# Transposing normalised rows by DMA instead of TensorE in a hybrid decoder step on eight cores

## The reference

```python
h = rmsnorm(x, g_mix);  proj = h @ w_in              # a | u | v | gate_a | gate_b
pa = pool_mixer(a)                                   # causal window means, 4 groups
u, v = gelu(u), rmsnorm(gelu(v), g_v)
sg = u * (tril(w_s) @ v + b_s)                       # per chunk of 128 rows
merged = sigmoid(gate_a) * (pa @ w_pool_out) + sigmoid(gate_b) * (sg @ w_gmlp_out)
x = x + merged @ w_out
h2 = rmsnorm(x, g_ffn)
x = x + (silu(h2 @ w_gate) * (h2 @ w_up)) @ w_down   # 2816 hidden
y = rmsnorm(x, g_final)
```

## Time and profile before

| what | value |
|---|---|
| median of 3 runs | 889.79 us (888.06 to 893.38) |
| span of the profiled execution, slowest core | 882.3 us (cores: 876.1 to 882.3) |
| PE busy | 830.3 us, 94% of the span |
| DVE / ACT / POOL busy | 366.0 / 247.1 / 142.6 us |
| PE share of the chain that ended last | 88% |
| DMA traffic | 81.05 MB, mean 92 GB/s |

### The profile page before, as it was taken

The page is one execution under the profiler, slowest core; times in us unless marked ns, Lnnn a source line. Parts: engine busy times, 40 slices in busy tenths (PEclk is TensorE's granted clock), DMA queues, the critical chain, the costliest instruction groups (busy, mean ns, idle before and its releaser), DMA issues.

```text
span 882.3 us, 13022 instructions; the slowest of 8 cores (876.1 to 882.3 us)
## 1 busy us (share of the span) xinstructions
PE 830.3 (94%) x4584; PEld 392.5 (44%) x4584; DVE 366.0 (41%) x601; ACT 247.1 (28%) x448; POOL 142.6 (16%) x174
## 2 busy tenths in 40 slices
PE   1689999999999999999997999999999999999996
PEld 1334444445444444444443444444544444444442
DVE  2448544447322211134557594434631212114446
ACT  3643422225311111120126543222441111110012
POOL 2420011021201010000225201201120101000003
PEclk9989999999999999999999999999999999999999
DMA  8995336666884746266367951567678475455304
GB/s 209 201 141 66 72 39 74 79 102 91 95 97 51 94 51 82 40 93 96 48 139 243 155 66 25 73 82 103 80 87 104 54 90 72 60 84 84 60 18 174
DMA packets 102482, 81.05 MB, mean 92 GB/s; under 512 B 5324, under 2 KB 96964, under 8 KB 102403
## 3 DMA queue, kind: packets, MB, share of 16 engines
q0 software_dynamic: 94048, 58.10, 51.6%
q1 hardware_dynamic: 7390, 20.88, 7.4%
q10 hardware_dynamic: 981, 1.24, 0.6%
HBM read 129.76 MB, written 9.01 MB: 157 GB/s over the span
## 4 chain that ended last, share of the span: by engine, by line
PE 88%; DMA 5%; DVE 3%; issue 1%; SPq 1%; ACT 1%; POOL 1%; DVEq 0%; POOLq 0%; ACTq 0%
PE ps L346 86%; DMA ring<-w_in 2%; DMA xbuf<-xs 2%; PE ps L396 1%; SPq L304 1%; DVE hb L384 1%; DVE ps L644 1%; ACT hT L404 0%; POOL rs L364 0%; DVE shr L536 0%; DVE shr L544 0%; DVE ovl L549 0%; DVE ovl L649 0%; PE ps L593 0%; DVEq L917 0%
## 5 line engine op out<-in xcount | busy, mean ns | idle before, releaser
L346 PE MATMUL ps<-hT,ring 128*128 128x512 bf16 (+1 forms) x2720 | 497.0, 338 | 7.4 <-DMA ring<-w_in 3.9
L346 PEld LDWEIGHTS ps<-hT,ring 128*128 128x128 bf16 x2720 | 228.0, 98 | 263.3 <-issue 11.5
L346 PE MATMUL ps<-ring,ovl 128*128 128x512 bf16 (+1 forms) x1020 | 224.3, 379 | 0.0
L739 DVE TENSOR_TENSOR ovl<-ftmp,ps 128x512 bf16<-128x512 f32 (+1 forms) x110 | 62.3, 583 | 248.4 <-PE ps L346 245.1
L346 PEld LDWEIGHTS ps<-ring,ovl 128*128 128x128 bf16 (+1 forms) x1020 | 97.7, 97 | 118.8 <-issue 4.3
L737 ACT ACTIVATE ftmp<-ps 128x512 f32<-128x512 f32 (+1 forms) x110 | 56.6, 514 | 246.2 <-PE ps L346 246.1
L355 ACT ACTIVATE junk<-xbuf 128x1024 bf16<-128x1024 f32 (+1 forms) x47 | 49.6, 1055 | 139.4 <-DVE xbuf L861 60.7
L364 POOL TENSOR_TENSOR rs<-ms,mhalf 128x1 f32<-128x1 f32 (+1 forms) x68 | 55.5, 819 | 176.4 <-DVE ms L360 176.4
L825 DVE TENSOR_TENSOR xbuf<-xbuf,ps 128x512 f32<-128x512 f32 (+1 forms) x68 | 46.7, 687 | 54.7 <-PE ps L346 54.7
L346 PE MATMUL ps<-ovl,ring 128*128 128x512 bf16 (+1 forms) x320 | 63.2, 337 | 0.0
L707 DVE TENSOR_TENSOR shr<-shr,ps 128x512 f32<-128x512 f32 (+1 forms) x40 | 23.4, 584 | 91.9 <-PE ps L346 91.9
(11 more groups left out here) (76 smaller groups left out, 378.9 us busy)
## 6 DMA issues: line engine op xcount, KB each, us to landing
ring<-w_gate POOLq DMA_DIRECT2D x22, 512.0 KB, 8.5
ring<-w_up POOLq DMA_DIRECT2D x22, 512.0 KB, 10.8
xbuf<-xp SPq DMA_DIRECT2D x16, 512.0 KB, 8.7
ring<-w_in POOLq DMA_DIRECT2D x16, 512.0 KB, 10.4
ring<-w_down POOLq DMA_DIRECT2D x8, 1024.0 KB, 10.2
ring<-w_in POOLq DMA_DIRECT2D x6, 1024.0 KB, 18.9
yp<-ybuf SPq DMA_DIRECT2D x11, 512.0 KB, 3.2
ring<-w_out POOLq DMA_DIRECT2D x4, 1024.0 KB, 13.4
```

Of the source, the lines that this page charges most:

```text
L346: ins = e.matmul(out=out, lhsT=lhs_fn(i), rhs=rhs_fn(i), start=(i == 0), stop=(i == n - 1))
L739: P.op('dve', lambda e: e.tensor_tensor(out=actT[:, f, c0:c0 + W], in0=ftmp[:, fi, :W], in1=PS[bU][:, :W], op=ALU.mult), reads=[('ftmp', f ...
```

## The change

Outside the head, `st_tr` becomes one transposing DMA transfer issued by SP, from `hb` straight into `hT`; PE, PSUM and ACT have no part in it. `hb` gets a third buffer, paid for by letting `nppbuf` share `vout`'s memory. In the FFN norm the sample slot goes first. In the first gate block all work on column chunk 0 now comes before chunk 1, and chunk 1 before the sample.

```diff
-        hb = sb("hb", [128, 2, D], BF16)
+        hb = sb("hb", [128, 3, D], BF16)
...
-        nppbuf = sb("nppbuf", [16, 512], F32)
+        nppbuf = vout
...
-        def norm_stages(slot, R, col0, grep, gres, copy_eng=None, src=None, src_res=None):
+        def norm_stages(slot, R, col0, grep, gres, by_dma=True, src=None, src_res=None):
...
             def st_h():
-                hi = nxt('hb', 2)
+                hi = nxt('hb', 3)
...
             def st_tr():
                 hi = box['hi']
+                dst = hT[:, :, col0:col0 + R]
+                if by_dma:
+                    P.dma('sp', (lambda e: e.dma_start_transpose(out=dst, in_=hb[:R, hi, :])), 'tr%d' % hi,
+                          reads=[('hb', hi)], writes=[('hT', slot, 0), ('hT', slot, 1)])
+                    return
                 b = bank()
...
-                pipeline([norm_stages(slot, R, col0, gmix_rep, 'gmix') for (slot, R, col0) in tts],
+                pipeline([norm_stages(slot, R, col0, gmix_rep, 'gmix', by_dma=False)
+                          for (slot, R, col0) in tts],
                          [0, 1, 2, 3])
...
-            for (slot, R, col0) in tts:
+            for (slot, R, col0) in (tts[8:] + tts[:8]):
                 def st_mm(slot=slot, R=R, col0=col0):
...
-                for fl in range(2):
-                    f = 2 * j + fl
-                    for ni, (c0, W, tl) in enumerate(nts):
-                        if j == 0 and fl == 0 and ni == 0:
-                            continue
-                        bG, bU = h_mm(gw, uw, hres, fl, c0, W, tl)
-                        h_evac(f, c0, W, bG, bU)
+                order = [(fl, ni) for fl in range(2) for ni in range(len(nts))]
+                if j == 0:
+                    order = sorted(order, key=lambda o_: o_[1])[1:]
+                for (fl, ni) in order:
+                    c0, W, tl = nts[ni]
+                    bG, bU = h_mm(gw, uw, hres, fl, c0, W, tl)
+                    h_evac(2 * j + fl, c0, W, bG, bU)
```

More of the change, by code:

```diff
@@ L400, in st_tr @@
                 src = PSB[b][:, :, :R]
[L401 to L408, removed]
+                P.op('act', lambda e: e.activation(out=dst, in_=src, func=AF.Copy),
+                     writes=[('hT', slot, 0), ('hT', slot, 1), ('ps', b)])
             return [st_sq, st_rs, st_h, st_tr]
@@ L570, in npp_ops @@
                                                                in_=PS[b][:15, 0:128], func=AF.Copy),
-                                 reads=[], writes=[('nppbuf', g), ('ps', b)])
+                                 reads=[], writes=[('nppbuf', g), 'vout', ('ps', b)])
                         if defer:
@@ L765, in st_mm @@
                              reads=[('x', slot, half)], writes=[('x', slot, half), ('ps', b)])
-                ns = norm_stages(slot, R, col0, gffn_rep, 'gffn', copy_eng='act')
+                ns = norm_stages(slot, R, col0, gffn_rep, 'gffn')
                 def st0(st_mm=st_mm, sq=ns[0]):
```

## The result

The changed kernel takes 913.26 us (median of 4, 912.84 to 913.98) against 890.12 (median of 4, 888.06 to 893.38): 2.9% slower, ratio 1.0295 with a 95% interval of 1.0253 to 1.0337. Forecast were 880.2, with 871 to 900 as the range.

What follows compares the result with a forecast made beforehand. The prediction took PE to bound the kernel, 88% of the chain. Removed 16.9 us, plus 1.7 for the sample and 5.6 for landing waits, gave -9.6: 889.8 to 880.2 us, range 871 to 900.

Steps and rivals of the forecast that it cites:

- The turns of slots 0 to 3: Second half's first norm: taking these four turns off PE removes 2.6 us, and nothing waits afterwards.
- The second half's FFN norm: PE's time there beyond its matmuls, lost to turns and their waits: 5.5 us removed.
- The wait for the sample: First half's FFN norm: with the sample first, PE waits once for DVE's last merge, 1.7 us added.
- L = 5 for the last slot: FFN norms: the last tile takes 5 us from written rows in hb to readable hT, being sent under load.
- the wait of L - 2.2: First gate block: PE waits before column chunk 1 for the last turned tile, 2.8 us per half, 5.6 in all.
- The upper bound, 6.4: Highest landing time in us for a turned tile, from 1,024 pieces at 77 ns over 16 engines plus a 1.5 floor.
- I cost this at nothing: Border of the halves: PE's waits for late turns of slots 4 to 7, 4 us uncovered, hidden by DVE and POOL.
- The gain of 3.6: Border of the halves: us saved by removing four turns, with DVE and POOL limiting it; ends 0 and 6.6.
- latency and clock: Rival: landing takes 8 us, waits 5.8 per half, TensorE's clock drop adds 3.4; 889.6 us, no change; chance 0.16.
- The queue that can't keep up: Rival: queue time per tile S reaches 4.9 us, tiles pile up, PE waits 15.4 per half; 905 us; chance 0.20.
- The hidden case: Rival: transfer lands within 2.2 us, no wait before chunk 1 of the first gate block; 874.6 us; chance 0.12.
- four signs of being wrong: Profile signs: landing times growing by slot, DVE waiting before st_h, clock near half after waits, PE idle late in stage C.

Runs made afterwards that it cites:

- e1: Changed kernel, but POOL's two w_out ring refills wait until slot 7's turned rows have landed; 890.4 to 892.6 us, ratio to before 1.0052.
- e10: Changed kernel with TensorE turning slots 4 to 7 at the border, sample last, refills waiting for slot 7's written rows; 873.92 us, ratio to before 0.9865.
- e6: e1, with POOL's refills behind w_down at the border also held until slot 7's turned rows have landed; 884.7 us, single run.
- e7: e1, with each border turn put on SP's queue right behind the step that writes its rows; 890.0 us, single run.
- e9: Changed kernel with TensorE at the border, FFN-norm refills waiting only for slot 7's written rows; first gate blocks 15.9 to 16.0 and 15.2 us.
- e8: Changed kernel with TensorE at the border and only the second FFN-norm refill held; first gate blocks 24.1 to 27.0 and 23.7 to 24.2 us.

## Why the prediction was wrong

**What was removed was sized right.** The turns of slots 0 to 3: forecast 2.6, measured 18.3 - 15.7 = 2.6. The second half's FFN norm: forecast 5.5 before any wait; e1 gives 2.7 + 1.4 = 4.1 with a wait of about 1.2 left. The first half's: 5.2 less 1.7 for the sample; e1 gives 3.2 + 0.6 - 1.9 = 1.9, with 1.15 of wait left; with the sample last and no wait, e10 gives 3.1 + 1.9 = 5.0 of the 5.2. The wait for the sample is 1.7 to the digit.

**Where the error is.** The forecast was -9.6, the stages give 28.7. Of the 38.3 between them 19.9 lie in the FFN norms (16.5 in place of -5.2 + 1.7 - 5.5 + 5.6 = -3.4) and 18.4 at the border (16.1 - 1.3 = 14.8 in place of -3.6).

**The term that failed first: L = 5 for the last slot, "the tile that matters goes out under load".** The mechanism was right, the wait of L - 2.2 in front of chunk 1 is there in both halves; L was 13.3 under load and not 5. The price came from a store that took 5.2 in a busy stretch, of which I took it that any transfer under load is slowed by a half or so. The upper bound, 6.4, was worked out from the price of pieces and had no waiting behind other transfers in it. The row that should have carried the upper bound was the refill itself, and the forecast had seen that POOL issues it first. The page of before:

```profile
ring<-w_gate POOLq DMA_DIRECT2D x22, 512.0 KB, 8.5
```

Two such loads go ahead of the turn, and the turn lands with the second. In the two stages this term was 11.5 + 10.6 in place of 5.6, and with the clock behind each wait, 19.2 of the 28.7 by stages.

**The term that failed second: "I cost this at nothing" at the border.** I had seen that the turns of slots 4 to 7 stand behind stores and loads on SP's queue, priced the delay at 4 us, and covered it by DVE and POOL. PE waited 18.4, and stage C took 16.1 more, so DVE and POOL covered next to nothing. e6 shows that POOL's refills are the main cause here too, e7 that a place further up SP's queue doesn't help while they run. How much SP's own stores and loads add to it is not settled. The gain of 3.6 that the forecast put there is in no kernel: with TensorE's turns the stage is as it was, with the DMA's it waits.

**The rivals.** Of the three the second, latency and clock, had the mechanism, with a wait of 5.8 per half where 11 came; its clock term is in the windows above (15 matmuls in 5 us, 0.64). The queue that can't keep up, which gave the nearest time (905), was wrong in its reason: S is about 1.3, landing times don't grow from slot to slot (in the second half's FFN norm they fall, from 10.2 for slot 0 to 3.0 for slot 3), and a quiet tile lands in 3.0. The hidden case was nearly true of every tile that had the engines to itself: what it lacked in the FFN norms was only who is issued first (e9).

Of the four signs of being wrong that the forecast named, three came: the clock behind the waits, PE idle in stage C, and DVE waiting in front of `st_h` for a transfer:

```profile
DVE hb L384 <- DMA hT<-hb: 4.3, 3, 2.6
```

The 2.6 are at the border, for slot 7's rows. In the second half's FFN norm DVE waits 0.9, since slots 0 to 2 land late (10.2, 7.6 and 6.7, behind loads issued 7.7 us and more earlier); that costs PE nothing, the stage takes the 27.6 that its matmuls need.

**The pages.** The 261 GB/s of the Trainium skill ("DMA: Bandwidth & Descriptors", the section on latency and other measured facts) meant an estimate of 1.0 us for a tile. The trace has 1.3 of engine time for a quiet tile, which is near it, and a landing at 3.0. The 1,309 ns per 128x128 block of the Trainium skill ("VectorE: DVE Perf Modes", the three transpose paths) is not a price to be multiplied: eight blocks land in 3.0 together. The rule of the Trainium skill that bears on the result is in the section on queues, rings and completion order of "DMA: Bandwidth & Descriptors": each DMA engine takes turns between the queues packet by packet. If a packet of the profile is one of those, which no run here shows, a tile of 66 packets per engine beside loads of 77 ns per packet and about 20 of its own (1.3 x 16 / 1,056) would need some 6.4 us (an estimate) and the fixed part; it took 13.3. Counted so, the trace doesn't bear that out as the whole mechanism; with another count of the packets it might.

**What stays open.** Why a tile issued 1.5 us behind the first load, through another queue, lands with the last load ahead of it, and one issued 0.6 ahead of the same loads loses nothing. The runs show that it is so, not what in the engines makes it so. At the border a turn issued ahead of POOL's loads was late as well (e7), and how much of that, and of the remaining 3.7 in e6, is SP's own stores and loads was not separated.

## What to carry to other kernels

Moving an on-chip turn from TensorE to the DMA engines removes its full time from TensorE (0.45 us a tile here), but gives it a latency that depends on what else is in those engines: 3.0 alone, 13.3 behind a refill's two loads. So look for the transfers of other queues that the same event releases, and see that the one on the critical path is issued first; a dependency that holds two refills for some 2 us (e9) takes 21 us out of the two first gate blocks here (26.9 + 25.4 to 16.0 + 15.2). Being first was enough where the queue had nothing else in flight. At the border, with stores and loads on the same queue, it was not, and holding the refills cost 4.9 in the stages behind (e6): there leave the turn on the engine.

## What the runs showed of the hardware

A transposing DMA of 128x1024 bf16 is 1,056 packets and lands in 3.0 us when alone. SP's time per issue is 1.2 then, 2.9 behind the refill and up to 9.6 at the border. Issued behind two 512 KB weight loads of GpSimd's, it landed in 13.3 on core 1, 0.5 behind the second load, and 0.2 to 0.8 behind it on all cores and in both halves of the changed kernel and of e8; an ordinary load of the same queue took 12.1. The two further loads that the changed kernel issues behind the turn, and e8 holds back, cost little (waits on core 5 of 8.4 and 8.9 with them, 8.4 and 8.5 without). Issued 0.6 ahead of the same four loads, it landed in 3.1.
